# Head of a one-core hybrid decoder kernel: squares on two engines, scaling in pieces of 256 columns, the conv state turned between the x tiles

## Chip, cores and metric

The kernel runs on one core of one Trainium2 chip. The metric is the device time in microseconds of one execution.

## The reference, cut to what matters

One layer for 512 prompt tokens and 64 sample tokens (8 sequences of 8), width 1024, all in float32. Only its first lines are touched by the change:

```
h = rmsnorm(x, norm1_w)             # x * rsqrt(mean(x*x) + eps) * w, per token
proj = h @ w_in                     # 1024 wide in, 9248 wide out
q, k, v, z, xbc, dt, ga, gb = split(proj)
xbc, conv_new = causal_conv(xbc, conv_state, conv_w, conv_b)   # needs the last 3 rows of 8 sequences, 3072 channels
...                                 # stick-breaking attention over the paged cache, SSD scan, gates,
...                                 # output projection, SwiGLU feed-forward
```

Each float32 product is computed as three products of split operands, hi times hi, hi times lo and lo times hi.

## The kernel before

Each engine has its own program; they meet only in semaphores. Tokens lie in five tiles: four of 128 prompt tokens (x0 to x3) and one of 64 sample tokens (x4), in `x_tok`. Products have weights as the stationary operand, in chunks of 128 output columns, and the whole x (`x_hi`, `x_lo`: 8 slices of 128 rows by 576 tokens) as the moving one, so all of x must be squared, scaled and turned before the first chunk of weights can be finished. That start is the part that the change touches.

- SyncE issues the loads of x0 to x4, then the chunks of w_in (512 KB each); chunk 2 waits until chunk 0 has been split (`split`).
- ScalarE first issues 13 small loads on its own DMA queue: nine of parameters (`par_in`), `d_rows`, two of `dt_par`, and the conv state `sc_rows` (24 rows of 3072). Then it loads its table, squares x0 to x4 with the sum along the row, and makes `stats[:, 2]`, the inverse root per token.
- VectorE scales each x tile by it (1024 columns in one instruction, `x_scaled`).
- TensorE turns the parameters, then the 24 slices of the conv state into two spare banks ("conv_in"), then x. For each k of 8 it turns slice k of the five tiles into two of the four spare banks (I call these five matmuls turn k), ScalarE makes `x_hi` and VectorE `x_lo` from the banks with the norm weight from `par`, and TensorE multiplies slice k-1 with chunk 0 (six matmuls, `first_tile`; I call them product k-1). Turn k+2 needs the banks of turn k. So one turn is under way while the one before is being split.
- `make_hi(c)` on ScalarE and `make_lo(c)` on VectorE split weight chunk c; tile c needs them.

After product 7 come tile 1 with chunk 1, and all the rest of the program (attention with the gate weights as filler, the SSD groups, output and feed-forward), which this change leaves as it is except for a shift by two in the turn of the four spare banks.

Of the kernel before, what the change touches and what calls it, by code (L numbers as in the profile page):

```python
# [16 lines left out]
ALU = mybir.AluOpType  # L17
ACT = mybir.ActivationFunctionType

P = 128  # L20
D = 1024
# [104 lines left out]
def build(nc, x_prompt, x_sample, cache_k, cache_v, page_table, state_ssm, state_conv, norm1_w, w_in,  # L126
# [32 lines left out]
    with ExitStack() as ctx:  # L159
# [231 lines left out]
        keys = [("par", 0), ("par", 1), ("conv_in", 0), ("conv_in", 1)]  # L391
# [341 lines left out]

        sem_const_first, sem_const_all = [], []
# [3 lines left out]
        def _(sp_eng):  # L738
# [10 lines left out]
            for c in range(N_FIRST):  # L749
                load_chunk(eng, first_src(c), c, width=P if c < N_FIRST - 1 else NH)  # L750
            eng.dma_start(pages_sb[:, :], page_table.rearrange("b p -> (b p)").rearrange("(o n) -> o n", o=1)).then_inc(sem("pages_in"), 16)
# [73 lines left out]
        def _(pool):  # L825
# [195 lines left out]
            eng.wait_ge(sem("picks_made"), 1)  # L1021
# [88 lines left out]
        def _(pe):  # L1110
# [4 lines left out]
            pe.wait_ge(sem("par_in"), 16 * 9)  # L1115
            pe.transpose(spare(("par", 0))[:, 0:5 * CT], par_rows[:, :], ident[0:5 * CT, 0:5 * CT]).then_inc(bank_full[use[("par", 0)][0]], 1)
            pe.wait_ge(sem("d_spread"), 1)
            pe.transpose(spare(("par", 1))[:, 0:50], par2_rows[:, :], ident[0:50, 0:50]).then_inc(bank_full[use[("par", 1)][0]], 1)
            pe.wait_ge(sem("conv_state_in"), 16)
            for j in range(2):  # L1120
                for n in range(12):
                    ct = 12 * j + n
                    mm = pe.transpose(spare(("conv_in", j))[:, 24 * n:24 * n + 24], sc_rows[:, ct * P:(ct + 1) * P], ident[0:24, 0:24])
                mm.then_inc(bank_full[use[("conv_in", j)][0]], 1)
# [20 lines left out]

# [569 lines left out]
        def _(act):  # L1715
            eng = act

            eng.dma_start(par_rows[0:CW * CT, :], conv_w[0].rearrange("w (t p) -> (w t) p", p=P)).then_inc(sem("par_in"), 16)
# [6 lines left out]
            eng.dma_start(d_rows[32:48, :], d_skip[0].rearrange("(j e) -> j e", e=2)).then_inc(sem("d_in"), 16)  # L1725
            eng.dma_start(dt_par[:, 0:1], dt_bias[0].rearrange("(h o) -> h o", o=1)).then_inc(sem("dt_par_in"), 16)
            eng.dma_start(dt_par[:, 1:2], a_log[0].rearrange("(h o) -> h o", o=1)).then_inc(sem("dt_par_in"), 16)
            eng.dma_start(sc_rows[:, :], state_conv[0].rearrange("b t c -> (b t) c")).then_inc(sem("conv_state_in"), 16)

# [3 lines left out]
            for c, t0, m in token_tiles():  # L1733
                eng.wait_ge(sem(f"x_in{c}"), 16)
                junk = qo[0:m, 2 * c:2 * c + 2, 0:512]
                eng.activation(junk, x_tok[0:m, c, :].rearrange("p (a b) -> p a b", a=2), ACT.Square,
                               accum_out=stats[0:m, 0, c:c + 1]).then_inc(sem("x_rms"), 1)
# [3 lines left out]
            eng.activation(stats[:, 2, :], stats[:, 1, :], ACT.Exp, scale=-0.5).then_inc(sem("x_rms"), 1)  # L1741
            make_hi(0)
# [5 lines left out]
            for j in range(2):  # L1748
                key = ("conv_in", j)
                wait_full(eng, key)  # L1750
                eng.activation(conv_in[:, 12 * j:12 * j + 12, :].rearrange("p t n -> p (t n)"), spare(key)[:, 0:288], ACT.Copy)\
                   .then_inc(bank_read[use[key][0]], 1)
# [52 lines left out]
            for c in range(N_FIRST):  # L1805
                make_hi(c + 1, width=NH if c + 1 == N_FIRST - 1 else P, after_tiles=c if c else None)
                if 1 <= c <= KD + 2:
# [183 lines left out]
            for pick in picks:  # L1991
# [4 lines left out]
               .then_inc(sem("picks_made"), 1)  # L1996
# [338 lines left out]
        def _(dve):  # L2335
# [9 lines left out]

            eng.wait_ge(sem("d_in"), 16)
            eng.tensor_copy(par2_rows[32:48, :].rearrange("j (e p) -> j e p", e=2), d_rows[32:48, :].unsqueeze(2).to_broadcast([16, 2, HD]))\
               .then_inc(sem("d_spread"), 1)
            eng.wait_ge(sem("x_rms"), 7)
            for c, t0, m in token_tiles():  # L2350
                eng.tensor_scalar(x_tok[0:m, c, :], x_tok[0:m, c, :], stats[0:m, 2, c:c + 1], None, ALU.mult).then_inc(sem("x_scaled"), 1)
            make_lo(0)
            for k in range(KD):
                for j in range(2):
                    key = ("x", k, j)
                    eng.wait_ge(sem("x_hi_made"), 2 * k + j + 1)
# [661 lines left out]
```

## Time and profile before

| | us |
|---|---|
| median of 3 runs (lowest, highest) | 1417.89 (1417.79, 1418.38) |
| the profiled execution | 1418.91 |
| its span from first to last instruction | 1417.4 |
| TensorE matmul busy | 1351.2 (95%) |
| VectorE busy | 963.0 (68%) |
| ScalarE busy | 707.4 (50%) |
| GpSimd busy | 263.5 (19%) |

The profiled execution is 1.0 us above the median, and 1.5 us of it lie outside the span. All times of rows are counted from the start of the span. TensorE is busy in nearly every slice after the first; it does nothing in the first 10 us.

### The profile page before, as it was taken

The page shows a single profiled execution, that of the slowest core. Times are in us where ns is not written, and L with a number is a line of the kernel's source. Part 1 is how long each engine was busy: PE and PEld are TensorE (multiplying, and loading weights), DVE is VectorE, ACT ScalarE, POOL GpSimd, SP SyncE. Part 2 cuts the span into 40 slices and gives each one's busy share as a digit, 9 for nine tenths or more (in the row PEclk, how much of TensorE's full clock was granted, in tenths as well). Part 3 has the DMA queues.
Part 4 walks back from the last instruction along what each step waited for, and adds up shares of the span by engine and source line. Part 5 has one row for each costly group of instructions (what it writes and reads, how often), then busy time and mean ns, then how long its engine had stood idle before and what let it go on. Part 6 is the DMA issues. An engine that isn't in the chain of part 4 may idle for free. (4 is left out here: it accounts for less than half of the span.)

```text
span 1417.4 us, 26926 instructions
## 1 busy us (share of the span) xinstructions
PE 1351.2 (95%) x10301; PEld 1257.5 (89%) x10301; DVE 963.0 (68%) x1569; ACT 707.4 (50%) x1271; POOL 263.5 (19%) x467
## 2 busy tenths in 40 slices
PE   5999999999999899999999999999999999999996
PEld 4998777899999898888888887899999999999996
DVE  4455546788853476787787776877899999983221
ACT  4576445777632354574464464535644444452221
POOL 4002233000021423333333324211100000000000
PEclk9999999999999999999999999999999999999998
DMA  4226665122255333334334425362333333323331
GB/s 122 75 77 193 180 209 163 56 71 71 71 159 166 75 86 109 95 96 116 107 95 124 109 68 176 111 204 75 90 90 90 104 105 90 90 71 98 97 95 36
DMA packets 200897, 152.86 MB, mean 108 GB/s; under 512 B 15529, under 2 KB 187585, under 8 KB 200720
## 3 DMA queue, kind: packets, MB, share of 16 engines
q1 hardware_dynamic: 175394, 97.93, 24.5%
q0 software_dynamic: 24992, 52.85, 12.7%
q8 instruction: 83, 1.36, 0.4%
q10 hardware_dynamic: 384, 0.37, 0.1%
q14 instruction: 44, 0.35, 0.1%
HBM read 127.80 MB, written 23.29 MB: 107 GB/s over the span
## 5 line engine op out<-in xcount | busy, mean ns | idle before, releaser
L487 PE MATMUL tile_banks<-x_hi,w_hi 128*128 128x288 f32 (+1 forms) x1232 | 368.1, 314 | 11.5 <-DVE w_lo L461 10.1
L488 PE MATMUL tile_banks<-x_lo,w_hi 128*128 128x288 f32 (+1 forms) x1104 | 309.7, 296 | 0.0
L491 PE MATMUL tile_banks<-x_hi,w_lo 128*128 128x288 f32 (+1 forms) x1232 | 262.4, 294 | 0.0
L487 PEld LDWEIGHTS tile_banks<-x_hi,w_hi 128*128 128x128 f32 (+1 forms) x1232 | 231.7, 188 | 25.2 <-DVE w_lo L461 12.4
L461 DVE TENSOR_TENSOR w_lo<-w_raw,w_hi 128x1024 fp32r<-128x1024 f32 (+2 forms) x125 | 150.5, 1204 | 113.0 <-ACT w_hi L455 112.4
L488 PEld LDWEIGHTS tile_banks<-x_lo,w_hi 128*128 128x128 f32 (+1 forms) x1104 | 207.7, 188 | 5.5 <-issue 3.6
L491 PEld LDWEIGHTS tile_banks<-x_hi,w_lo 128*128 128x128 f32 (+1 forms) x1232 | 197.5, 187 | 0.4
L455 ACT ACTIVATE w_hi<-w_raw 128x1024 fp32r<-128x1024 f32 (+2 forms) x125 | 129.5, 1036 | 99.2 <-PE tile_banks L491 94.0
L488 PE MATMUL tile_banks<-f_lo,w_hi 128*128 128x288 f32 x352 | 98.6, 294 | 0.0
L1102 POOL DMA_DIRECT2D out_y_prompt<-y_tok x8 | 6.2, 778 | 386.1 <-ACT y_tok L2315 373.3
L2203 ACT ACTIVATE w_hi<-sum_raw 128x512 fp32r<-128x512 f32 x71 | 44.9, 634 | 60.3 <-PE tile_banks L1674 24.6
L488 PEld LDWEIGHTS tile_banks<-f_lo,w_hi 128*128 128x128 f32 x352 | 66.1, 188 | 0.0
L2572 DVE SCALAR_TENSOR_TENSOR conv_acc<-conv_src,conv_par,conv_acc 128x600 f32<-128x600 f32 x72 | 62.1, 862 | 2.5
L886 POOL DMA_DIRECT2D v_page<-in_cache_v x64 | 34.4, 537 | 154.4 <-issue 154.4
L487 PE MATMUL tile_banks<-y_hi,w_hi 128*128 128x288 f32 x192 | 56.1, 308 | 0.3 <-DVE w_lo L461 0.3
L487 PE MATMUL tile_banks<-t_blocks,w_hi 128*128 128x288 f32 x192 | 54.7, 300 | 1.6 <-DVE f_lo L2931 1.5
L488 PE MATMUL tile_banks<-y_lo,w_hi 128*128 128x288 f32 x192 | 53.8, 295 | 0.0
L2836 DVE TENSOR_TENSOR w_lo<-sum_raw,w_hi 128x512 fp32r<-128x512 f32 x71 | 49.9, 703 | 5.5 <-ACT w_hi L2203 5.5
L2031 ACT ACTIVATE conv_src<-tile_banks 128x288 f32<-128x288 f32 x24 | 9.9, 411 | 87.2 <-PE tile_banks L491 87.2
L2437 DVE TENSOR_TENSOR_SCAN after_w<-rest,zero_col 128x128 f32<-128x128 f32 (+2 forms) x64 | 52.3, 817 | 0.3
L1064 POOL DMA_DIRECT2D out_ssm_sample<-old x32 | 25.5, 797 | 118.1 <-DVE old L2717 108.0
L2439 DVE TENSOR_TENSOR beta<-beta,after_w 128x512 f32<-128x512 f32 (+2 forms) x80 | 42.6, 532 | 2.8
(490 smaller groups left out, 3678.1 us busy)
## 6 DMA issues: line engine op xcount, KB each, us to landing
w_raw<-in_w_in SPq DMA_DIRECT2D x68, 512.0 KB, 4.0
k_page<-in_cache_k SPq DMA_DIRECT2D x64, 128.0 KB, 2.6
v_page<-in_cache_v POOLq DMA_DIRECT2D x64, 128.0 KB, 3.0
old<-in_state_ssm POOLq DMA_DIRECT2D x32, 256.0 KB, 3.5
out_ssm_sample<-old POOLq DMA_DIRECT2D x32, 256.0 KB, 2.9
w_raw<-in_w_pb SPq DMA_DIRECT2D x16, 512.0 KB, 3.5
w_raw<-in_w_down SPq DMA_DIRECT2D x16, 512.0 KB, 4.0
gates_dram<-gate_out POOLq DMA_DIRECT2D x22, 288.0 KB, 2.8
```

Source lines behind the costliest of these rows:

```text
L455: nc.scalar.activation(w_hi[:, c % 2, 0:tiles, 0:width], w_raw[:, c % 2, 0:tiles, 0:width], ACT.Copy).then_inc(hi_made, 1)
L461: nc.vector.tensor_tensor(w_lo[:, c % 2, 0:tiles, 0:width], w_raw[:, c % 2, 0:tiles, 0:width], f32(w_hi[:, c % 2, 0:tiles, 0:width]), ALU. ...
L487: nc.tensor.matmul(out, wh, xh[:, HALVES[h]], start=start and k == 0, stop=False, skip_group_check=onto)
L488: nc.tensor.matmul(out, wh, xl[:, HALVES[h]], start=False, stop=False, skip_group_check=onto)
L491: mm = nc.tensor.matmul(out, wl, xh[:, HALVES[h]], start=False, stop=stop and k == last, skip_group_check=onto)
L886: eng.dma_start(v_page[:, n % V_SLOTS, :], cache_v[0, bass.ds(page_of(eng, x, k), 1)].rearrange("o p h d -> p (o h d)")).then_inc(sem(f"v_ ...
L1064: eng.dma_start(states_of(ssm_sample, g, b), old[:, b % 2]).then_inc(sem(f"state_stored{b % 2}"), 16)
L2203: eng.activation(form_slot(f)[0], form_raw(f), ACT.Copy).then_inc(sem("form_hi_made"), 1)
L2437: link(eng.tensor_tensor_scan(out=after_w[:, slot, edge - width:edge][:, ::-1], data0=rest[:, slot, cols][:, ::-1], data1=zero_col[:, 0:1] ...
L2439: return eng.tensor_tensor(beta[:, x["u"] % 4, cols], beta[:, x["u"] % 4, cols], after_w[:, slot, edge - width + 1:edge + 1], ALU.mult)
L2572: ins = eng.scalar_tensor_tensor(out=dst, in0=src[:, w:w + m], scalar=conv_par[:, w * CT + ct:w * CT + ct + 1], in1=dst, op0=ALU.mult, op1 ...
L2836: eng.tensor_tensor(low, form_raw(f), f32(high), ALU.subtract).then_inc(sem("form_split"), 1)
```

## The change

ScalarE squares x0, x2, x4 and VectorE x1, x3. Scaling is cut in pieces of 256 columns (two slices): pieces of x3 and x4 on ScalarE, of x0 to x2 on VectorE, the first ones before turn 0, the next ones after slices 0, 2 and 4 have been split. Turn 0 comes before the parameters' turns. The conv state's turns go to the idle product banks `G[1]`, four behind each of turns 2 to 7; their copies to `conv_in` stand behind the split of chunk 1, and tile 1 waits for them. The loads of the conv state and of `dt_par` move from ScalarE's queue to SyncE's, behind weight chunk 1, and `d_rows` becomes ScalarE's first load. One semaphore is replaced by another count of an existing one.

```
             for c in range(N_FIRST):
                 load_chunk(eng, first_src(c), c, width=P if c < N_FIRST - 1 else NH)
+                if c == 1:
+                    eng.dma_start(sc_rows[:, :], state_conv[0].rearrange("b t c -> (b t) c")).then_inc(sem("conv_state_in"), 16)
+                    eng.dma_start(dt_par[:, 0:1], ...).then_inc(sem("dt_par_in"), 16)
+                    eng.dma_start(dt_par[:, 1:2], ...).then_inc(sem("dt_par_in"), 16)
...
@@ TensorE @@
+            def turn_conv_state(cts):
+                pe.wait_ge(sem("conv_state_in"), 16)
+                for ct in cts:
+                    n = ct % 12
+                    mm = pe.transpose(conv_state_bank(ct // 12)[:, 24 * n:24 * n + 24], sc_rows[:, ct * P:(ct + 1) * P], ident[0:24, 0:24])
+                    if n == 11:
+                        mm.then_inc(sem("conv_state_turned"), 1)
...
-                        if k == 0:
-                            pe.wait_ge(sem("x_scaled"), c + 1)
+                        if k % 2 == 0:
+                            pe.wait_ge(sem("x_scaled"), 5 * (k // 2 + 1))
...
+                if k == 0:
+                    turn_par()
+                if k >= 2:
+                    turn_conv_state(range(4 * (k - 2), 4 * (k - 1)))
                 if k:
                     first_tile(k - 1)
             first_tile(KD - 1).then_inc(tile_done, 1)
+            pe.wait_ge(sem("conv_state_in"), CONV_STATE_READ)
...
@@ ScalarE @@
             for c, t0, m in token_tiles():
+                if c not in SQUARES_ACT:
+                    continue
...
+            def scale_columns(k):
+                for c, t0, m in token_tiles():
+                    if c in SCALED_ACT:
+                        cols = slice(k * P, k * P + SCALE_COLS)
+                        eng.activation(x_tok[0:m, c, cols], x_tok[0:m, c, cols], ACT.Copy, scale=stats[0:m, 2, c:c + 1]).then_inc(sem("x_scaled"), 1)
+            eng.wait_ge(sem("x_rms"), 7)
+            scale_columns(0)
             make_hi(0)
...
+                if k % 2 == 0 and k + 2 < KD:
+                    scale_columns(k + 2)
...
@@ VectorE @@
+                if c in SQUARES_DVE:
+                    eng.wait_ge(sem(f"x_in{c}"), 16)
+                    eng.scalar_tensor_tensor(out=qo[...], in0=x_tok[0:m, c, :], scalar=1.0, in1=x_tok[0:m, c, :],
+                                             op0=ALU.mult, op1=ALU.mult, accum_out=stats[0:m, 0, c:c + 1]).then_inc(sem("x_rms"), 1)
...
-                eng.tensor_scalar(x_tok[0:m, c, :], x_tok[0:m, c, :], stats[0:m, 2, c:c + 1], None, ALU.mult).then_inc(sem("x_scaled"), 1)
+                        eng.tensor_scalar(x_tok[0:m, c, cols], x_tok[0:m, c, cols], stats[0:m, 2, c:c + 1], None, ALU.mult).then_inc(sem("x_scaled"), 1)
```

TensorE, from its first instruction to the first products. Before:

```order
L1116 MATMUL spare_bank<-ident,par_rows 128x120 [waits par_in,constants]
L1118 MATMUL spare_bank<-ident,par_rows 128x50 [waits d_spread]
L1123 MATMUL spare_bank<-ident,sc_rows 128x24 [waits conv_state_in]
L1123 MATMUL spare_bank<-ident,sc_rows 128x24 x23
L1140 MATMUL spare_bank<-ident,x_tok 128x128 [waits x_scaled,bank_read0]
```

Of the change, the same place, and on to product 1:

```order
L1157 MATMUL spare_bank<-ident,x_tok 128x128 [waits x_scaled,constants]
L1157 MATMUL spare_bank<-ident,x_tok 128x128 [waits x_scaled] x3
L1157 MATMUL spare_bank<-ident,x_tok 128x64 [waits x_scaled]
L1131 MATMUL spare_bank<-ident,par_rows 128x120 [waits par_in]
L1133 MATMUL spare_bank<-ident,par_rows 128x50 [waits d_spread]
...
L1157 MATMUL spare_bank<-ident,x_tok 128x128 [waits x_scaled,bank_read2]
L1157 MATMUL spare_bank<-ident,x_tok 128x128 [waits x_scaled] x3
L1157 MATMUL spare_bank<-ident,x_tok 128x64 [waits x_scaled,bank_read3]
L1139 MATMUL tile_banks<-ident,sc_rows 128x24 [waits conv_state_in]
L1139 MATMUL tile_banks<-ident,sc_rows 128x24 x3
L487 MATMUL tile_banks<-x_hi,w_hi 128x288 [waits weights_split,bank_read1,bank_read0]
```

The 24 turns of the conv state left the place ahead of turn 0; four stand now between a turn and the product behind it, six times.

ScalarE, from the table load to the second slice. Before:

```order
L1731 ACT_TABLE_LOAD
L1736 ACTIVATE qo,stats<-x_tok 128x2x512 [waits x_in0,constants]
...
L1741 ACTIVATE stats<-stats 128x5 [waits x_rms]
L455 ACTIVATE w_hi<-w_raw 128x1024 [waits weights_in0]
L1747 ACTIVATE conv_par<-spare_bank 128x120 [waits bank_full0]
L1747 ACTIVATE par<-spare_bank 128x50 [waits bank_full1]
L1751 ACTIVATE conv_in<-spare_bank 128x288 [waits bank_full2]
L1751 ACTIVATE conv_in<-spare_bank 128x288 [waits bank_full3]
L1759 ACTIVATE x_hi<-spare_bank,par 128x512 [waits bank_full0,bank_read1]
```

Of the change:

```order
L1761 ACTIVATE stats<-stats 128x5 [waits x_rms]
L1767 ACTIVATE x_tok<-x_tok,stats 128x256 [waits x_rms]
L1767 ACTIVATE x_tok<-x_tok,stats 64x256
L455 ACTIVATE w_hi<-w_raw 128x1024 [waits weights_in0]
L1776 ACTIVATE conv_par<-spare_bank 128x120 [waits bank_full0]
L1776 ACTIVATE par<-spare_bank 128x50 [waits bank_full1]
L1783 ACTIVATE x_hi<-spare_bank,par 128x512 [waits bank_full2,bank_read1]
L1783 ACTIVATE x_hi<-spare_bank,par 128x64 [waits bank_full3]
L1767 ACTIVATE x_tok<-x_tok,stats 128x256
L1767 ACTIVATE x_tok<-x_tok,stats 64x256
L1783 ACTIVATE x_hi<-spare_bank,par 128x512 [waits bank_full0]
```

Two scaling pieces stand now ahead of the first weights and two behind the first slice; the copies of the conv state are gone from here.

## Rows read from the trace of the kernel before

**Rows 1.** The page, its head line.
```profile
span 1417.4 us, 26926 instructions
```
**Rows 2.** Loads of x3 and x4 (issue starts; issue to landing, least and most).
```profile
L741 SPq DMA_DIRECT2D x_tok<-in_x_prompt x1: 432/432/432, 2.5 to 2.5; - x1
L742 SPq DMA_DIRECT2D x_tok<-in_x_sample x1: 568/568/568, 2.9 to 2.9; - x1
...
DMA to landing us min/median/max: 7.8/8.5/9.2
```
**Rows 3.** Load of weight chunk 0, the same columns.
```profile
L445 SPq DMA_DIRECT2D w_raw<-in_w_in x1: 594/594/594, 3.5 to 3.5; - x1
...
DMA to landing us min/median/max: 12.0/12.0/12.0
```
**Rows 4.** Timeline of ScalarE in the head (start us, us, engine, line, what).
```profile
5.12 0.76 ACTq L1726 DMA_DIRECT2D dt_par<-in_dt_bias  x1
...
7.13 1.28 ACT L1731 ACT_TABLE_LOAD   x1 [7.13 <-issue]
...
12.60 1.04 ACT L1736 ACTIVATE qo<-x_tok 64x1024 fp32r<-64x1024 f32 x1
...
15.57 1.06 ACT L455 ACTIVATE w_hi<-w_raw 128x1024 fp32r<-128x1024 f32 x1 [1.27 <-DMA w_raw<-in_w_in]
...
16.69 0.20 ACT L1747 ACTIVATE par<-spare_bank 128x50 f32<-128x50 f32 x1
16.78 0.41 ACT L1751 ACTIVATE conv_in<-spare_bank 128x288 f32<-128x288 f32 x1
...
18.92 0.89 ACT L1759 ACTIVATE x_hi<-spare_bank,par 128x512 fp32r<-128x512 f32 x2 [0.69 <-PE spare_bank L1140]
```
**Rows 5.** Timeline of VectorE in the head.
```profile
14.34 3.39 DVE L2351 TENSOR_SCALAR x_tok<-x_tok,stats 128x1024 f32<-128x1024 f32 x5 [2.25 <-ACT stats L1741]
...
19.64 0.94 DVE L2359 SCALAR_TENSOR_TENSOR x_lo<-spare_bank,par,x_hi 128x512 fp32r<-128x512 f32 x2 [0.78 <-ACT x_hi L1759]
```
**Rows 6.** Timeline of TensorE's weight loads, conv state to product 2.
```profile
15.02 2.63 PEld L1123 LDWEIGHTS spare_bank<-ident,sc_rows 24*128 24x128 f32 x24 [2.71 <-DMA sc_rows<-in_state_conv]
17.70 0.71 PEld L1140 LDWEIGHTS spare_bank<-ident,x_tok 128*128 128x128 f32 x4
...
20.65 0.29 PEld L487 LDWEIGHTS tile_banks<-x_hi,w_hi 128*128 128x128 f32 x1 [0.39 <-DVE x_lo L2359]
...
22.06 0.85 PEld L1140 LDWEIGHTS spare_bank<-ident,x_tok 128*128 128x128 f32 x4
...
23.43 0.19 PEld L487 LDWEIGHTS tile_banks<-x_hi,w_hi 128*128 128x128 f32 x1
...
24.21 0.49 PEld L1140 LDWEIGHTS spare_bank<-ident,x_tok 128*128 128x128 f32 x4
24.87 0.14 PEld L1140 LDWEIGHTS spare_bank<-ident,x_tok 64*128 64x128 f32 x1 [0.17 <-issue]
25.07 0.19 PEld L487 LDWEIGHTS tile_banks<-x_hi,w_hi 128*128 128x128 f32 x1
```
**Rows 7.** Timeline, slice 4 on its way to product 4.
```profile
26.61 0.89 ACT L1759 ACTIVATE x_hi<-spare_bank,par 128x512 fp32r<-128x512 f32 x2 [0.74 <-PE spare_bank L1140]
...
27.33 0.94 DVE L2359 SCALAR_TENSOR_TENSOR x_lo<-spare_bank,par,x_hi 128x512 fp32r<-128x512 f32 x2 [0.69 <-ACT x_hi L1759]
...
28.35 0.19 PEld L487 LDWEIGHTS tile_banks<-x_hi,w_hi 128*128 128x128 f32 x1
```
**Rows 8.** Timeline, from the split of chunk 1 to tile 1.
```profile
32.31 1.06 ACT L455 ACTIVATE w_hi<-w_raw 128x1024 fp32r<-128x1024 f32 x1
...
33.60 1.22 DVE L461 TENSOR_TENSOR w_lo<-w_raw,w_hi 128x1024 fp32r<-128x1024 f32 x1
...
34.87 0.19 PEld L487 LDWEIGHTS tile_banks<-x_hi,w_hi 128*128 128x128 f32 x1 [0.77 <-DVE w_lo L461]
```
**Rows 9.** Busy time by stretch: PE, PEld, DVE, ACT, POOL, granted clock, DMA share, GB/s.
```profile
478.00:482.00 4.00, 4.00 (x23) 4.00 (x23) 0.00 (x0) 0.22 (x1) 3.07 (x7) 0.68 0.70 163
```

More of the change, by code:

```diff
@@ L388, in build @@
         gates_dram = nc.dram_tensor("gates_dram", (N_FILL, P, T), F32, kind="Internal").ap()
-        keys = [("par", 0), ("par", 1), ("conv_in", 0), ("conv_in", 1)]
+        keys = [("par", 0), ("par", 1)]
         keys += [("x", k, j) for k in range(KD) for j in range(2)]
@@ L732, in f_low, with conv_state_bank @@
             return f_lo[:, k, :]
+        SCALE_COLS = 2 * P
+        SQUARES_ACT, SQUARES_DVE = (0, 2, 4), (1, 3)
+        SCALED_ACT, SCALED_DVE = (3, 4), (0, 1, 2)
+        CONV_STATE_READ = 16 + 2
+        def conv_state_bank(j):
+            return G[1][:, j, 0:12 * 24]
         sem_const_first, sem_const_all = [], []
@@ L750, in _ @@
                 load_chunk(eng, first_src(c), c, width=P if c < N_FIRST - 1 else NH)
+                if c == 1:
+                    eng.dma_start(sc_rows[:, :], state_conv[0].rearrange("b t c -> (b t) c")).then_inc(sem("conv_state_in"), 16)
+                    eng.dma_start(dt_par[:, 0:1], dt_bias[0].rearrange("(h o) -> h o", o=1)).then_inc(sem("dt_par_in"), 16)
+                    eng.dma_start(dt_par[:, 1:2], a_log[0].rearrange("(h o) -> h o", o=1)).then_inc(sem("dt_par_in"), 16)
             eng.dma_start(pages_sb[:, :], page_table.rearrange("b p -> (b p)").rearrange("(o n) -> o n", o=1)).then_inc(sem("pages_in"), 16)
@@ L1020, in _ @@
                 sums_in(st)
-            eng.wait_ge(sem("picks_made"), 1)
+            eng.wait_ge(sem("sums_hi_made"), 3)
             for g in range(2):
@@ L1113, in _, with turn_par @@
             pe.wait_ge(sem("constants"), sem_const_first[0])
[L1115 to L1124, printed above, removed]
+            def turn_par():
+                pe.wait_ge(sem("par_in"), 16 * 9)
+                pe.transpose(spare(("par", 0))[:, 0:5 * CT], par_rows[:, :], ident[0:5 * CT, 0:5 * CT]).then_inc(bank_full[use[("par", 0)][0]], 1)
+                pe.wait_ge(sem("d_spread"), 1)
+                pe.transpose(spare(("par", 1))[:, 0:50], par2_rows[:, :], ident[0:50, 0:50]).then_inc(bank_full[use[("par", 1)][0]], 1)
+            def turn_conv_state(cts):
[5 more added lines that the diff above has]
+                        mm.then_inc(sem("conv_state_turned"), 1)
             def first_tile(k):
@@ L1716, in _ @@
             eng = act
+            eng.dma_start(d_rows[32:48, :], d_skip[0].rearrange("(j e) -> j e", e=2)).then_inc(sem("d_in"), 16)
             eng.dma_start(par_rows[0:CW * CT, :], conv_w[0].rearrange("w (t p) -> (w t) p", p=P)).then_inc(sem("par_in"), 16)
@@ L1724, in _ @@
                     eng.dma_start(par2_rows[at:at + 1, e * HD:(e + 1) * HD], w).then_inc(sem("par_in"), 16)
[L1725 to L1728, printed above, removed]
             eng.preload_act_table_set("natural_log_exp_and_others")
@@ L1733, in _ @@
             for c, t0, m in token_tiles():
+                if c not in SQUARES_ACT:
+                    continue
                 eng.wait_ge(sem(f"x_in{c}"), 16)
-                junk = qo[0:m, 2 * c:2 * c + 2, 0:512]
+                junk = qo[0:m].rearrange("p a t -> p (a t)")[:, c * D:(c + 1) * D].rearrange("p (a b) -> p a b", a=2)
                 eng.activation(junk, x_tok[0:m, c, :].rearrange("p (a b) -> p a b", a=2), ACT.Square,
@@ L1747, in _ @@
                 eng.activation(dst[:, :], spare(key)[:, 0:n], ACT.Copy).then_inc(bank_read[use[key][0]], 1)
[L1748 to L1752, printed above, removed]
             wait_after_read(eng, ("par", 1))
@@ L1806, in _ @@
                 make_hi(c + 1, width=NH if c + 1 == N_FIRST - 1 else P, after_tiles=c if c else None)
+                if c == 0:
+                    for j in range(2):
+                        eng.wait_ge(sem("conv_state_turned"), j + 1)
+                        eng.activation(conv_in[:, 12 * j:12 * j + 12, :].rearrange("p t n -> p (t n)"), conv_state_bank(j), ACT.Copy)\
+                           .then_inc(sem("conv_state_in"), 1)
                 if 1 <= c <= KD + 2:
@@ L1995, in _ @@
             eng.activation(pair_picks[used, :].rearrange("p (e d) -> p e d", e=2), pair_rows[used, 0:2].unsqueeze(2).to_broadcast([SEG_ROWS, 2, HD]), ACT.Copy)\
-               .then_inc(sem("picks_made"), 1)
+               .then_inc(sem("sums_hi_made"), 1)
             def conv_silu(key):
@@ L2344, in link, with scale_columns @@
                 eng.wait_ge(chain, n_chain[0])
+            eng.wait_ge(sem("constants"), sem_const_first[0])
+            for c, t0, m in token_tiles():
+                if c in SQUARES_DVE:
+                    eng.wait_ge(sem(f"x_in{c}"), 16)
+                    eng.scalar_tensor_tensor(out=qo[0:m].rearrange("p a t -> p (a t)")[:, c * D:(c + 1) * D], in0=x_tok[0:m, c, :], scalar=1.0,
+                                             in1=x_tok[0:m, c, :], op0=ALU.mult, op1=ALU.mult,
+                                             accum_out=stats[0:m, 0, c:c + 1]).then_inc(sem("x_rms"), 1)
+            def scale_columns(k):
+                for c, t0, m in token_tiles():
+                    if c in SCALED_DVE:
+                        cols = slice(k * P, k * P + SCALE_COLS)
+                        eng.tensor_scalar(x_tok[0:m, c, cols], x_tok[0:m, c, cols], stats[0:m, 2, c:c + 1], None, ALU.mult).then_inc(sem("x_scaled"), 1)
+            eng.wait_ge(sem("x_rms"), 7)
+            scale_columns(0)
             eng.wait_ge(sem("d_in"), 16)
@@ L2348, in _ @@
                .then_inc(sem("d_spread"), 1)
-            eng.wait_ge(sem("x_rms"), 7)
-            for c, t0, m in token_tiles():
-                eng.tensor_scalar(x_tok[0:m, c, :], x_tok[0:m, c, :], stats[0:m, 2, c:c + 1], None, ALU.mult).then_inc(sem("x_scaled"), 1)
             make_lo(0)
@@ L2360, in _ @@
                                              in1=f32(x_hi[:, k, cols]), op0=ALU.mult, op1=ALU.subtract).then_inc(bank_read[use[key][0]], 1)
+                if k % 2 == 0 and k + 2 < KD:
+                    scale_columns(k + 2)
             wait_after_read(eng, ("par", 1))
```

## Prediction

> **What bounds the kernel now.** I read the page first, then the timeline of the first 40 us engine by engine, then the landings of single loads. The span is 1417.4 us [rows 1], and TensorE is busy nearly all of it once it has begun, so a microsecond by which tile 1 starts earlier is a microsecond of the whole, and only the time up to tile 1, which starts at 34.87 [rows 8], is at stake. I call the five x turns of slice k "turn k" and the six matmuls of first_tile(k) "product k", as above.
>
> Three chains meet there. (a) ScalarE loads its table at 7.13, behind its DMA issues, and squares five tiles back to back at 1.04 each; the last starts at 12.60, and scaling can start 1.74 later, at 14.34; VectorE needs 3.39 for it, to 17.73 [rows 4, 5]. (b) TensorE waits for the conv state until 15.02 and turns it in 2.63, and begins turn 0 at 17.70, so (a) and (b) end together [rows 5, 6]. (c) Weight chunk 0 lands at 3.5 + 12.0 = 15.5, is split to hi at 15.57 [rows 3, 4]. Then x_hi of slice 0 starts at 18.92, x_lo at 19.64, and product 0 at 20.65 [rows 4 to 6].
>
> From there a loop: product 0 starts at 20.65, product 1 at 23.43, product 2 at 25.07, product 4 at 28.35 [rows 6, 7], which is 1.64 each; so product 7 is at 28.35 + 3 x 1.64 = 33.27, and tile 1 follows 1.6 later behind the low part of chunk 1 (1.22) [rows 8]. Two things set the 1.64 at once. TensorE has 0.78 for a product (23.43 to 24.21) and 0.86 for a turn (24.21 to 25.07) [rows 6], together all of it. And a slice takes from turn to product 24.21 to 26.71, 2.5 us (a turn's start to x_hi about 0.77, x_hi to x_lo 0.72, x_lo to product 1.02 [rows 6, 7]); with the 0.78 of the product ahead of the turn that is 3.28 for two slices. So TensorE has no free time in the loop: whatever is put in there is paid.
>
> **The change, part by part.** *Start of scaling.* Three DMA issues leave ScalarE, so the table load moves from 7.13 to 5.12, and it ends at 6.4 [rows 4]. Three squares then wait for data, not for the engine. The last needs x4, which landed at 2.9 + 9.2 = 12.1, though x3, twice its size, landed at 2.5 + 7.8 = 10.3 [rows 2]. The conv state and dt loads that now shared the DMA engines with it come after it. Bounds: 12.1, nothing gained, and 10.3, with x3. I take 11.0. Scaling starts 1.74 later, 12.75. VectorE's squares of x1 and x3 are not in the trace; 0.94 for 576 columns [rows 5] makes at most 1.7 for 1024, so the one of x3 is over at 12.0, covered by x4's 1.04 and the roots; if x4 came with x3 it would be late by some 0.6.
>
> *First pieces.* VectorE, three of 256 columns: a whole tile takes 3.39/5 = 0.68, a quarter of it 0.17 without overhead; I take 0.25 each, 0.75. ScalarE, two: 288 columns took 0.41 [rows 4], so at most 0.8. Turn 0 starts at 13.5, 4.2 before the old one.
>
> *To product 0.* Turn 0 takes 1.37 at the slow clock (22.06 to 23.43), then the parameters' two turns, two matmuls where turn 0 has five, so 0.55, and a gap: 15.6. ScalarE copies them (0.20 for par), so x_hi at 15.85 and product 0 by 1.73 later (18.92 to 20.65 [rows 4, 6]): 17.6. The other chain is chunk 0: landing, 1.06, 1.22, 1.01 and small gaps. It must land by 14.2 not to bind. It landed at 15.5 behind the same competitors; I take 13.5. With 15.5 product 0 would be at 18.9. So product 0 gains 3.0, bounds 1.7 and 4.2.
>
> *The conv turns.* 24 turns in 2.63, 0.11 each at the slow clock [rows 6]. Ahead of turn 0 they go away (part of the 3.0). Behind turns 2 to 7 four stand each time in a loop without slack. Their price at the full clock is unknown: product and turn went from 1.41 (20.65 to 22.06) and 1.37 to 0.78 and 0.86 [rows 6], so 0.055 to 0.11 each, 0.22 to 0.44 for four; and the change from 128-row to 64-row turns costs a gap of 0.17 (24.87) [rows 6], which 64 to 24 rows may cost again. Per loop 0.2 to 0.6; I take 0.35: 0.07 a turn and half of the gap, for a group that may overlap its neighbours. The first comes ahead of product 1, at the slow clock, 0.6. The loss up to product 7 is 0.6 and four times 0.35 (turns 3 to 6; that behind turn 7 delays product 6, which has 0.8 to spare), 2.0; bounds 1.2 and 3.0.
>
> *The clock.* Matmuls are at half rate (1.2 GHz) in product 0 and turn 2, and at the full rate (2.4) from product 1 on [rows 6]: 1.41 against 0.78 for the same six. Before the rise there had been turns from 15.02 and products from 20.65; it came between 22.06 and 23.43, some 2.5 us after the first product. If it again follows the products by 2.5 it comes at 20.1, when turn 2 is about over: product 0 at 17.6, turn 2 at 19.0, conv turns 20.4, product 1 at 21.0, gain 2.4, of which the slow clock takes nothing more. If it follows the turns (8.1 after 15.02, so 21.6 after a start at 13.5), product 1 is mostly slow, 0.4 lost. If it stays at 23.2, product 1 and turn 3 are slow, 0.6 + 0.5 = 1.1 lost. I take the first. The Trainium skill (TensorE: Matmul & The Clock Gate, Part 4: PE-mode transpose) says that transposes don't count as TensorE being busy; by that rule the rise goes with the products, the sum as above, against 0.4 less if turns counted. The trace agrees in that 5 us of turns did not raise it.
>
> *Scaling pieces in the loop.* VectorE 0.75 behind x_lo of slices 0, 2, 4: it idles 0.69 there [rows 7] and the loop is now 0.35 longer. ScalarE 0.75, idle 0.74 [rows 7], the same. Turn k+2 comes after product k, 0.78 after x_lo, when the pieces are done. Nothing, up to 0.1 each if the loop were not longer.
>
> *The rest.* The conv copies, 2 x 0.41, stand behind the hi part of chunk 1 (32.31 to 33.37) and end at 34.2, 0.65 before tile 1 [rows 4, 8], which waits for them: nothing; they would cost at 1.5 each. SyncE's three issues more stand ahead of chunk 2, which waits for the split of chunk 0 anyway. The shift in the banks and the semaphore count cost nothing: the spare banks are used in the same turn with the same distances.
>
> **Sum.** +3.0 at product 0, less 0.6 ahead of product 1 and 1.4 in the loop: gain 1.0. The profiled execution's 1418.9 would become 1417.9; against the median, 1.0 below it, 1417.89 becomes 1416.9.
>
> **The rivals.**
> - *B, the loads come much earlier:* x4 at 10.3 or before, chunk 0 by 13, turns at 0.055 without a gap. Product 0 gains 4.2, the loop takes 1.2: gain 2 to 3.4, 1415.9 to 1414.5. For it: x4 is half a tile and landed 1.8 behind x3 [rows 2]. Against: SyncE's own weights stand right behind x4 in its queue.
> - *C, the loads come as before:* x4 at 12.1, chunk 0 at 15.5. Product 0 gains 1.7, the loop takes 2.0 less what its clock, at the same distance from the products, gives back at the edge of turn 2: gain 0 within 0.4, 1417.9. The change's sense would be lost. For it: whatever is behind x4 now was not proved to be the conv state.
> - *D, slower:* the clock does not rise by the end of the first short products, because they are now spread between turns, at 3.4 or more instead of 2.8 us. A rise at 23.2 takes 1.1, and the conv groups at 0.6 another 4 x 0.25 = 1.0: 1.0 - 1.1 - 1.0 = -1.1, so 1419.0. The sign turns with a rise at about 23.2; each further microsecond at the slow clock costs about 0.45 (1.41 against 0.78), so beyond 0.2% it needs a rise after 27.
> - *E, 478 to 482:* TensorE has a granted clock of 0.68 there after an idle stretch [rows 9], about 1.3 us lost. If the earlier arrival moves that stretch it may go or grow: 1415.6 or 1418.2.
>
> **How the numbers follow.** Forecast (gain 0.3 to 1.8) 0.50, B 0.26, C 0.11, D 0.09, E 0.04. 0.2% is 2.84 us, about what a measurement of this kernel can tell from no change. Of B half is beyond it, 0.13, with a little of E: faster 0.15. Of D a third: slower 0.03. Same 0.82. The range leaves out the upper part of B and the far part of D: 1415.0 to 1418.5.
>
> **What would show it.** Table load at about 5.1; last square at 11.0 (step 1 right) or 12.1 (C); turn 0 at 13.5; product 0 at 17.6; products 2.0 apart instead of 1.64 (the conv turns); full rate from 20 on; product 7 at about 32.3, tile 1 at 33.9. Wrong if the loop stays at 1.64 (then the gain is 2.5 or more), or if tile 1 waits for the conv copies.

## The result, and the profile after

The kernel after the change takes 1425.05 us (median of 7 runs, 1423.81 to 1429.29), the one before 1417.89 (7 runs, 1416.74 to 1420.20). The ratio is 1.0052, with a 95% interval of 1.0041 to 1.0063: **slower by 0.5%**, where 1416.9 was forecast, with 0.03 for slower. The profiled execution took 1424.49 with the span below, 5.6 us more than before [rows 1]. Single executions of before and of experiments 7, 8 and 10 took 1497 to 3608 us, where all others of one kernel lie within 12 us of each other; the ratios leave them out. The page of after, its head line:

```profile
span 1423.0 us, 26946 instructions
```

Timeline of ScalarE in the head of after (start, us, engine, line, what); it answers to [rows 4]:

```profile
5.22 1.28 ACT L1749 ACT_TABLE_LOAD   x1 [5.22 <-issue]
...
11.02 1.06 ACT L1756 ACTIVATE qo<-x_tok 64x1024 fp32r<-64x1024 f32 x1 [2.29 <-DMA x_tok<-in_x_sample]
...
12.77 0.91 ACT L1767 ACTIVATE x_tok<-x_tok,stats 128x256 f32<-128x256 f32 x2
13.58 1.04 ACT L455 ACTIVATE w_hi<-w_raw 128x1024 fp32r<-128x1024 f32 x1
...
16.15 0.89 ACT L1783 ACTIVATE x_hi<-spare_bank,par 128x512 fp32r<-128x512 f32 x2
```

All of this came close to the forecast: the square of x4 at 11.0 (11.0), the first pieces at 12.77 (12.75), x_hi of slice 0 at 16.15 (15.85). The timeline of TensorE's weight loads in after, which answers to [rows 6 to 8]; the rows shown are the first of product 0, turn 2, the first conv turns, products 1, 2 and 7, and tile 1:

```profile
17.88 0.29 PEld L487 LDWEIGHTS tile_banks<-x_hi,w_hi 128*128 128x128 f32 x1 [0.70 <-DVE x_lo L2404]
...
19.29 0.85 PEld L1157 LDWEIGHTS spare_bank<-ident,x_tok 128*128 128x128 f32 x4
20.47 0.18 PEld L1157 LDWEIGHTS spare_bank<-ident,x_tok 64*128 64x128 f32 x1 [0.33 <-issue]
20.77 0.50 PEld L1139 LDWEIGHTS tile_banks<-ident,sc_rows 24*128 24x128 f32 x4
21.32 0.29 PEld L487 LDWEIGHTS tile_banks<-x_hi,w_hi 128*128 128x128 f32 x1
...
24.76 0.29 PEld L487 LDWEIGHTS tile_banks<-x_hi,w_hi 128*128 128x128 f32 x1
...
39.89 0.33 PEld L487 LDWEIGHTS tile_banks<-x_hi,w_hi 128*128 128x128 f32 x1
...
41.33 0.33 PEld L487 LDWEIGHTS tile_banks<-x_hi,w_hi 128*128 128x128 f32 x1
...
42.05 0.27 PEld L488 LDWEIGHTS tile_banks<-x_lo,w_hi 128*128 128x128 f32 x1
...
42.53 0.19 PEld L487 LDWEIGHTS tile_banks<-x_hi,w_hi 128*128 128x128 f32 x1
42.66 0.19 PEld L488 LDWEIGHTS tile_banks<-x_lo,w_hi 128*128 128x128 f32 x1
```

Product 0 is 2.77 earlier than before (20.65 to 17.88), product 1 still 2.11 (23.43 to 21.32). Then products stand 3.44 apart until the end of the loop: 21.32 + 5 x 3.44 = 38.52 for product 6. A product takes 1.41 (17.88 to 19.29), as product 0 did before [rows 6]: TensorE stays at its low level, 1.2 GHz, through the whole loop in this execution. Only in the middle of tile 1, when products follow one another without turns, do the starts go from 0.24 to 0.13 apart (42.53 to 42.66), which is the 2.4 GHz level. Tile 1 starts at 41.33, 6.46 later than before [rows 8].

The sum of the rows is exact: +2.77 at product 0, -0.66 ahead of product 1, -8.73 from product 1 to product 7 (18.57 for 9.84), and +0.16 from product 7 to tile 1 (1.44 for 1.60), is -6.46. Busy time by stretch, in after, the columns of [rows 9]:

```profile
17.80:21.30 3.50, 3.38 (x15) 2.92 (x15) 1.65 (x6) 1.52 (x5) 1.38 (x4) 1.00 0.44 116
21.30:39.80 18.50, 18.50 (x81) 15.89 (x81) 7.51 (x21) 7.34 (x17) 0.00 (x0) 1.00 0.00 1
```

In 18.5 us the profile shows no idle time of TensorE's matmuls (18.50 of 18.50; their ends are modelled, and the weight loads have one gap of 0.33 in each slice), and still it runs at the low level. The column of the granted clock prints 1.00 there: ahead of the first rise it doesn't show the level, and one has to read it from the spacing of equal instructions. After the first rise it does show falls.

What is lost in the head is most of the difference. The gate and gated outputs leave on POOL's queue; of these groups of DMA issues (least, median and most ns, then first to last issue), first two of before, then two of after:

```profile
L905 POOL DMA_DIRECT2D gates_dram<-gate_out x22: 540/542/569, 133.1 to 401.6; - x22
L935 POOL DMA_DIRECT2D gated_dram<-gate_out x8: 544/546/552, 416.9 to 457.9; - x8
```

```profile
L918 POOL DMA_DIRECT2D gates_dram<-gate_out x22: 540/542/569, 139.8 to 407.8; - x22
L948 POOL DMA_DIRECT2D gated_dram<-gate_out x8: 544/544/549, 422.4 to 462.6; - x8
```

The lateness is 6.7 at 133, 6.2 at 402, 5.5 at 417, 4.7 at 458 and 5.6 at the end. So up to 1.8 of the 6.5 us are taken up on the way, and 0.9 of the span in the end. These are two single executions, and experiment 1 shows that one execution can gain or lose 2 to 3 us behind the head.

### The profile page after: what moved, and what is told of

Its sections match the earlier page's. It is cut to its first block and busy times, and to the rows that moved or that the text cites. A ratio compares the mean times of both kernels' runs of the same rounds, so it can differ in the third digit from the quotient of the medians.

```text
span 1423.0 us, 26946 instructions
## 1 busy us (share of the span) xinstructions
PE 1359.3 (96%) x10301; PEld 1264.6 (89%) x10301; DVE 965.8 (68%) x1580; ACT 708.5 (50%) x1275; POOL 263.9 (19%) x467
```

## The experiments

**Theory 1**, formed from the profile above: the conv turns lengthen the slow slice from 2.78 [rows 6] to 3.44, of which only 1.41 is products, and the clock doesn't rise in such a loop. **Theory 2:** it is the unbroken stretch of turns right ahead of product 0 (15.02 to 20.65 before) that lets the clock rise soon after, and the change took it away. **Theory 3:** the scaling pieces or the short last square are what slows the loop. "Constants" below are fp32 matmuls of the tile of ones by the identity into an unused part of a bank, whose result nobody reads; all conv turns are still made.

**Experiment 1: all conv turns behind the loop.** The rest of the change stays.

```
-                if k >= 2:
-                    turn_conv_state(range(4 * (k - 2), 4 * (k - 1)))
...
             first_tile(KD - 1).then_inc(tile_done, 1)
+            turn_conv_state(range(0, 24))
```

> The change, with all 24 conv turns behind product 7 instead of four behind each of turns 2 to 7. Theory 1 (the conv turns thin out the products so far that the clock does not rise in the loop): the clock rises within 2 to 6 us of product 0 at about 17.9, tile 1 starts between 32 and 35, and the time is 1415 to 1418.5. Theory 2 (what raised the clock before was the long unbroken run of turns ahead of product 0, which the change took away): the clock stays low through the loop, period 2.8, tile 1 at about 39 to 41, 1422 to 1425. Theory 3 (the scaling pieces and their waits in the loop) says the same as theory 2.

Measured: 1419.42 (12 runs, 1415.86 to 1423.38, in two groups, up to 1418.2 and from 1420.7), beside 1417.82 of before; ratio 1.0013 (1.0001 to 1.0024). The profiled execution took 1416.2. Its timeline of weight loads (product 7, the conv turns, tile 1):

```profile
30.45 0.19 PEld L487 LDWEIGHTS tile_banks<-x_hi,w_hi 128*128 128x128 f32 x1 [0.81 <-DVE x_lo L2403]
...
31.45 1.55 PEld L1139 LDWEIGHTS tile_banks<-ident,sc_rows 24*128 24x128 f32 x24 [0.16 <-issue]
33.60 0.19 PEld L487 LDWEIGHTS tile_banks<-x_hi,w_hi 128*128 128x128 f32 x1 [0.60 <-ACT conv_in L1835]
```

Product 1 came 2.89 behind product 0 (17.46 to 20.35), the clock rose within it, 3.6 behind product 0, and stayed up for the loop; product 7 stands at 30.45, 9.4 earlier than in after. So neither the missing turns ahead of product 0 (theory 2) nor the scaling pieces (theory 3) hold it down: both are as in after here. But the clock falls again, in the windows of the same kernel:

```profile
31.00:34.60 3.60, 3.10 (x35) 2.83 (x35) 1.68 (x2) 1.87 (x4) 0.00 (x0) 1.00 0.40 104
34.60:38.00 3.40, 3.40 (x17) 3.40 (x15) 1.23 (x1) 0.47 (x1) 0.00 (x0) 0.50 0.27 69
```

What TensorE did ahead of the fall was 24 conv turns and some idle time (31.45 to 33.60). Through it all of the 1.3 us by which tile 1 is earlier than before is gone: the first matmuls on `conv_out` start at 41.41, in before at 41.18. The clock and tile 1 came as theory 1 expected, the median (1415 to 1418.5) didn't. What separates the two groups is not shown, since the traced execution has this fall and lies in the lower group; its 2.7 us less than before's traced one come from behind the head.

**Experiment 2: only the conv turns' move, in the kernel before.** Squares, scaling and loads as before; the turns go into the loop by the line that experiment 1 takes out, and the copies of conv_in behind make_hi(1).

> The kernel before, with the conv turns alone moved as in the change (four behind each of turns 2 to 7, copies behind the split of chunk 1); squares, scaling and loads as before. Theory 1: product 0 at about 20, the clock stays low, period 3.44, tile 1 at about 42 to 43.5, 1425 to 1428. Theory 2: the same direction, since here too the 24 turns ahead of turn 0 are gone. Theory 3: the clock rises by 24, product to product 1.9, 1418 to 1420.

Measured: 1427.03 (1425.36 to 1428.41), ratio 1.0064 (1.0052 to 1.0076). This part alone costs at least what the whole change does; the medians lie 2 us apart, and the intervals overlap. Weight loads (product 0, conv turns, product 1):

```profile
19.24 0.29 PEld L487 LDWEIGHTS tile_banks<-x_hi,w_hi 128*128 128x128 f32 x1 [0.48 <-DVE x_lo L2364]
...
22.13 0.50 PEld L1124 LDWEIGHTS tile_banks<-ident,sc_rows 24*128 24x128 f32 x4
22.68 0.29 PEld L487 LDWEIGHTS tile_banks<-x_hi,w_hi 128*128 128x128 f32 x1
```

Again 3.44 apart, and the low level until about 44.9, by the spacing. Tile 1 is at 42.69.

**Experiment 3: after, with 24 constants ahead of turn 0.**

```
             pe.wait_ge(sem("constants"), sem_const_first[0])
+            for n in range(24):
+                pe.matmul(G[1][:, 0, 0:128], ones[:, :], ident[:, :])
```

> The change, with 24 float32 matmuls of constants (ones by ident, 128x128, into an idle bank, never read) in TensorE's idle time ahead of turn 0. If the clock is all that went wrong, turns 0 and 1 and all products run at the full rate: product 0 at 17.0 to 17.5, products about 1.9 to 2.0 apart, tile 1 at 31.5 to 33, time 1413.5 to 1416.5. If the share of products in the loop is also too small to keep the clock up, it falls again within the loop and tile 1 comes after 36.

Measured: 1426.28 (1424.33 to 1427.79), ratio 1.0055 (1.0043 to 1.0067): no gain. Its weight loads and windows:

```profile
3.42 7.71 PEld L1128 LDWEIGHTS tile_banks<-ident,ones 128*128 128x128 f32 x48 [3.42 <-POOL conv_out L848]
13.68 0.42 PEld L1159 LDWEIGHTS spare_bank<-ident,x_tok 128*128 128x128 f32 x4 [2.55 <-DVE x_tok L2392]
...
15.16 0.72 PEld L1159 LDWEIGHTS spare_bank<-ident,x_tok 128*128 128x128 f32 x4 [0.29 <-ACT conv_par L1778]
```

```profile
15.00:18.40 3.40, 2.78 (x11) 2.29 (x11) 3.21 (x8) 2.69 (x8) 2.76 (x11) 0.51 0.38 101
```

The constants raised the clock: four turn loads take 0.42 at 13.68, for 0.71 at the low level [rows 6]. Then TensorE waited 2.55 and made turns, and at 15.0 the clock was down (0.51), ahead of product 0. So the loop started at the low level, with its slices 3.44 apart; the expectation had the clock fall within the loop at the earliest. A clock that is high early is worth nothing if turns and idle time stand between it and the products.

**Experiment 4: half of the conv turns in the loop.** Two behind each of turns 2 to 7, twelve behind product 7.

> The change, with two conv turns behind each of turns 2 to 7 and twelve behind product 7. The slow loop would be about 3.2 us a slice instead of 3.44. Theory 1: between the two: either the clock rises late in the loop (tile 1 at 35 to 38, 1418 to 1422) or not at all (tile 1 at about 40, 1423 to 1425). Theory 2 and 3: as the change, 1423 to 1425.

Measured: 1426.81 (1424.78 to 1432.08), ratio 1.0069 (1.0051 to 1.0086). Slices of 3.23, tile 1 at 42.28, low until about 48.2; tile 1 and the time lie above both expected ranges. Two turns were enough to keep the clock down; that the 12 behind product 7 moved its rise from 42.2 to 48.2 fits experiment 1.

**Experiment 5: two constants more in each loop of after.** The slice grows, but by matmuls.

```
                 if k >= 2:
+                    for n in range(2):
+                        pe.matmul(G[1][:, 1, 288:416], ones[:, :], ident[:, :])
                     turn_conv_state(range(4 * (k - 2), 4 * (k - 1)))
```

> The change with all its conv turns in the loop, and two more float32 matmuls of constants (128x128, never read) ahead of each group of four. This makes the slow loop longer still (about 4.0 us a slice) but gives products about half of TensorE's time again, as in the kernel before. Theory 1 in its form 'what counts is the share of products, turns do not count': the clock rises in the loop, within 6 us of product 0, in spite of the longer loop. Theory 1 in its form 'a loop longer than so much keeps it down', or if anything that makes TensorE do more between products is bad: the clock stays low, tile 1 at 44 or later, 1428 or more.

Measured: 1426.01 (4 runs, 1422.24 to 1426.34), ratio 1.0052 (1.0037 to 1.0067); the profiled execution took 1422.24. Its weight loads around the rise (constants, conv turns, product 2, product 3):

```profile
24.97 0.93 PEld L1163 LDWEIGHTS tile_banks<-ident,ones 128*128 128x128 f32 x4
26.12 0.32 PEld L1139 LDWEIGHTS tile_banks<-ident,sc_rows 24*128 24x128 f32 x4 [0.23 <-issue]
26.48 0.19 PEld L487 LDWEIGHTS tile_banks<-x_hi,w_hi 128*128 128x128 f32 x1
...
29.11 0.19 PEld L487 LDWEIGHTS tile_banks<-x_hi,w_hi 128*128 128x128 f32 x1
```

The clock rose at 26.1, in the loop, 8.6 behind product 0 (expected: within 6), although product 2 stands 4.40 behind product 1 (22.08). So in this execution the clock rose in a longer slice than that of after, with more matmuls that aren't turns in it. The constants cost 0.64 a slice at the high level too (2.63 for the 1.99 of experiment 9), so the rise gives little back: 1422.24 beside 1424.49. But the other three executions took 3.5 to 4.1 more and have no trace. An estimate: a clock that stays low from product 2 to product 6 costs 7.1 (four slices at 4.40 for 2.63), so they fit a rise about two slices later, which is not shown.

**Experiments 6 to 8: other places for the 24 turns.** 6 puts six behind each of turns 4 to 7; 7 puts 12 ahead of product 0 and 12 behind product 7, into a spare bank; 8 puts all 24 ahead of product 0, behind turn 1. The line that changes, in 6, 7 and 8 in turn:

```
+                if k >= 4:
+                    turn_conv_state(range(6 * (k - 4), 6 * (k - 3)))
...
+                if k == 1:
+                    turn_conv_state(range(0, 12))
...
+                if k == 1:
+                    turn_conv_state(range(0, 24))
```

> The change with the conv turns put behind turns 4 to 7 only, six each, when the clock should be up already. If a thin loop only prevents the rise: the clock rises at 21 to 24 and stays, period about 2.1 at the full rate, tile 1 at 33 to 34.5, 1416 to 1418.5. If it also takes the clock down again once it is up: a fall between 26 and 35, tile 1 after 35, 1419 to 1424.

> The change with 12 conv turns in TensorE's idle time ahead of product 0 and 12 in its idle time ahead of tile 1, these into a spare bank so that tile 1 does not wait for their copy. Theory 1: product 0 at 18.4 to 18.8, clock up at 21 to 24 and no fall after product 7, tile 1 at 32 to 33, 1415 to 1416.5. If the clock falls behind product 7 as in the run with 24 there: 1417 to 1421, in two groups.

> The change with all 24 conv turns between turn 1 and product 0, none in the loop. Theory 1: product 0 at about 19.8, clock up within 2 to 5 us of it, tile 1 at 33.5 to 34.5, 1416 to 1418. No group of slow executions, since nothing stands between product 7 and tile 1.

Measured (12 runs each, before 1418.65): 1418.37, ratio 1.0001 (0.9987 to 1.0015); 1418.45, 1.0002 (0.9991 to 1.0013); 1419.28, 1.0001 (0.9991 to 1.0011). All are level with before. Tile 1 starts at 35.20, 35.90 and 35.03, later than expected in all three, and the medians of 7 and 8 lie above their ranges. Experiment 6 shows best what theory 1 says; its weight loads, and a window over slices with six turns each:

```profile
27.74 0.44 PEld L1139 LDWEIGHTS tile_banks<-ident,sc_rows 24*128 24x128 f32 x6
28.21 0.19 PEld L487 LDWEIGHTS tile_banks<-x_hi,w_hi 128*128 128x128 f32 x1
```

```profile
24.00:36.00 12.00, 11.26 (x87) 9.78 (x87) 7.73 (x19) 6.87 (x16) 0.00 (x0) 1.00 0.01 1
```

Products 0 to 2 have no conv turns ahead of them; they start 2.89 apart at first, and the clock rises among them, between 22.93 and 23.80. Six turns a slice then cost 0.46 (2.10 for 1.64) and don't bring it down: a loop with more turns than that of after, which couldn't raise the clock, keeps it up. In 7, whose slow slices are as short (2.89), it rose only at 27.9, 9.4 behind product 0, as its weight loads show (product 3 and turn 5):

```profile
27.17 0.29 PEld L487 LDWEIGHTS tile_banks<-x_hi,w_hi 128*128 128x128 f32 x1
...
28.27 0.49 PEld L1157 LDWEIGHTS spare_bank<-ident,x_tok 128*128 128x128 f32 x4
```

In 8 it rose at 24.4, 4.3 behind; before, some 2.5 behind. So even the short slice raises it after a time that varies. The traced executions of 7 and 8 also show a fall of some 3.4 us later on (from about 420.5 and 174.2), at places where no kernel here was changed.

**Experiment 9: the change as it is, with constants right up to product 0.**

```
+            constants(32)
...
+                if k == 1:
+                    constants(4)
                 if k >= 2:
```

> The change as it is, conv turns in the loop, with 32 float32 matmuls of constants ahead of turn 0 (up to about 13.5) and four in TensorE's idle time ahead of product 0. Theory 1, with what the run with the turns behind turns 4 to 7 showed (once up, the clock stays up in a thin loop): clock up at 7 to 11, no fall before tile 1, product 0 at 17.0 to 17.4, slices about 1.95 apart, tile 1 at 31.5 to 33, time 1414 to 1417: all of the change's loss is the clock. If it falls ahead of product 0 as in the run with 24 constants: 1424 to 1427 again.

Measured: 1417.06 (12 runs, 1413.82 to 1419.35), at the upper end of what was expected, beside 1418.9 of before; ratio 0.9984 (0.9973 to 0.9995). Its weight loads (constants, product 0, conv turns, products 1 and 2):

```profile
15.66 0.97 PEld L1131 LDWEIGHTS tile_banks<-ident,ones 128*128 128x128 f32 x8
16.73 0.19 PEld L487 LDWEIGHTS tile_banks<-x_hi,w_hi 128*128 128x128 f32 x1
...
18.36 0.32 PEld L1146 LDWEIGHTS tile_banks<-ident,sc_rows 24*128 24x128 f32 x4
18.72 0.19 PEld L487 LDWEIGHTS tile_banks<-x_hi,w_hi 128*128 128x128 f32 x1
...
20.71 0.19 PEld L487 LDWEIGHTS tile_banks<-x_hi,w_hi 128*128 128x128 f32 x1
```

With the clock up from the start the change's own loop runs at 1.99 a slice, product 7 is at 29.97 and tile 1 at 31.59, 9.7 earlier than in after. The two kernels differ in nothing but the constants: the way from a ratio of 1.0052 to one of 0.9984 is the clock's. That is 9.6 us, as the 9.7 of tile 1; the medians lie 8.0 apart, but each stands beside other runs of before (1417.89 and 1418.9). The change kept warm is 1.8 us faster than before, which starts at the low level itself, and 2.2 faster than before kept warm (experiment 10, by the medians).

**Experiment 10: the kernel before, kept warm in the same way** (38, 3 and 2 constants in its gaps).

> The kernel before with the same idea and nothing else: 38 float32 matmuls of constants ahead of the parameters' turns, three behind the conv turns, two ahead of product 0. Clock up from 7 to 11 on; product 0 at about 20, slices 1.64 apart, tile 1 at 32.5 to 33.5, 1415.5 to 1417: a gain of 1.5 to 2.5 without any part of the change.

Measured: 1419.3 (12 runs, 11 of them 1416.23 to 1424.07), ratio 1.0007 (0.9994 to 1.002). The profiled execution took 1416.33, 2.6 less than that of before; product 0 is at 20.10 and tile 1 at 33.15, 1.7 earlier. The head came as expected, and the median shows nothing of it. There is one hint: the mean granted clock is 0.996 in the traced execution, which has the clock up from the constants on, and 0.991 to 0.992 in the three slowest (1422.48 to 1424.07), where before has 0.993 to 0.996. That points to falls elsewhere in these executions, but where they are is not shown, and the execution of 1419.9 has 0.991 as well.

**Experiment 11: the split turns of 7, kept warm** (32 constants ahead of turn 0, two behind the 12 conv turns).

> The change with its conv turns split (12 ahead of product 0, 12 ahead of tile 1) and 32 constants ahead of turn 0, two ahead of product 0. Clock up from 7 to 11 on and not down again; product 0 at about 17.2, slices 1.64 apart, tile 1 at 30.3 to 31.5, 1412.5 to 1415: 3 to 5 us faster than the kernel before. If the clock falls ahead of product 0: 1418 to 1421.

Measured: 1415.64 (12 runs), ratio 0.9979 (0.9966 to 0.9991). The profiled execution took 1418.09, and in it the clock fell once more ahead of product 0 (18.91; tile 1 at 33.17), the case for which 1418 to 1421 was expected; the first conv turns, and the window:

```profile
17.05 1.00 PEld L1146 LDWEIGHTS tile_banks<-ident,sc_rows 24*128 24x128 f32 x12 [0.71 <-DMA sc_rows<-in_state_conv]
```

```profile
16.00:21.00 5.00, 4.43 (x29) 4.06 (x28) 2.84 (x8) 2.18 (x6) 2.47 (x9) 0.66 0.42 110
```

Ahead of it TensorE had waited 0.71 for the conv state, now behind the first weights in its queue, and made 12 turns.

**Experiment 12: late turns, kept warm.** Constants as in 9 (34 and 4), six conv turns behind turns 6 and 7 each, twelve behind product 7 in a spare bank as in 7.

```
+                if k >= 6:
+                    turn_conv_state(range(6 * (k - 6), 6 * (k - 5)))
```

> The change with 34 constants ahead of turn 0 and four ahead of product 0, its conv turns six each behind turns 6 and 7 and twelve ahead of tile 1 in a spare bank. If the clock is the whole story: up at 7 to 11 and no fall before tile 1, product 0 at 16.7 to 17.3, slices 1.64 apart up to product 4, tile 1 at 30 to 31, 1412.5 to 1415.5, the fastest of all. If a loop of 1.64 has hidden costs in the early start: tile 1 as in the run with four turns each, 31.6, 1417.

Measured: **1414.46** (10 runs, 1413.38 to 1416.11), beside 1417.6 of before; ratio 0.9978 (0.9969 to 0.9988). It has the lowest median and the narrowest runs; by the ratio it is level with experiment 11. Its weight loads (first constants, product 0, product 7, the last conv turns, tile 1):

```profile
3.43 9.54 PEld L1131 LDWEIGHTS tile_banks<-ident,ones 128*128 128x128 f32 x68 [3.43 <-POOL conv_out L848]
...
17.20 0.19 PEld L487 LDWEIGHTS tile_banks<-x_hi,w_hi 128*128 128x128 f32 x1
...
29.15 0.19 PEld L487 LDWEIGHTS tile_banks<-x_hi,w_hi 128*128 128x128 f32 x1 [0.34 <-DVE x_lo L2419]
...
30.14 0.82 PEld L1177 LDWEIGHTS spare_bank<-ident,sc_rows 24*128 24x128 f32 x12 [0.17 <-issue]
30.99 0.19 PEld L487 LDWEIGHTS tile_banks<-x_hi,w_hi 128*128 128x128 f32 x1
```

Tile 1 starts 3.9 earlier than before [rows 8]; of the span 4.0 are gone (1413.4), in the median 3.1.

## Why the prediction was wrong

**Up to product 0 it held.** Table load 5.22 (forecast 5.12), the last square 11.02 (11.0), scaling 12.77 (12.75), ScalarE's pieces 0.91 (at most 0.8), VectorE's 0.90 (0.75), product 0 at 17.88 (17.6): a gain of 2.77 for the 3.0 forecast. Chunk 0 didn't bind: its split followed the pieces at once, at 13.58 (13.5). That the sum came out this close is in part luck: the same head starts the square of x4 at 10.51 to 11.76 and product 0 at 17.46 to 18.64 in the traces of after and of experiments 1, 4, 5 and 6.

**The conv turns' price held too.** At the low level four cost 0.55 (20.77 to 21.32; forecast 0.6), and at the high level 0.35 (experiment 9: 1.99 for 1.64; forecast 0.35). Between the 64-row turn and the 24-row turns no gap is shown: the row at 20.77 in after has no idle time ahead of it. Over the loop with the clock up, from product 1 to product 7, they cost 11.25 (18.72 to 29.97) less the 9.84 of before, 1.41; forecast 1.4.

**The step that failed** is the one on the clock, "I take the first": a rise at 20.1, 2.5 us behind product 0, as before. It didn't come until 42.1. Of the 8.73 lost between products 1 and 7, 1.41 are the turns and the other 7.32 the low level. The argument took the distance from the first product to the rise as fixed, and so counted the turns as free for the clock, where they stretch the time between products. What decided, in these traces, was what stood between the products: with 1.41 of products in slices of 2.78 (before) and 2.89 (1, 6, 7, 8) the clock rose within the loop; with 1.41 in 3.23 (4) and in 3.44 (after, 2, 3) it didn't, in some 22 us; with constants added to the products it rose even in a slice of 4.40 (5, in the one execution that was traced). That the turns themselves count for nothing, or for less, is the reading which fits all of these, but a direct comparison of turns with equally long idle time wasn't run.

The forecast had weighed a rule against the rows here: the Trainium skill (TensorE: Matmul & The Clock Gate, Part 4: PE-mode transpose) says that transposes don't count as TensorE being busy in the same way. The runs agree with it, after's 18.5 us without idle time above all; the mistake was to use it only for when the rise would come, and not for whether it would.

**Rival D had the mechanism**, "the clock does not rise by the end of the first short products, because they are now spread between turns", with a chance of 0.09 and a loss of 1.1, for a rise at 23.2. Both were too low. (It also says that the sign turns with a rise at about 23.2; by its own sum the change is 1.1 slower there already.) For a later rise it gave a rate, 0.45 a microsecond, and the latest rise that it names is 27; by that rate a rise at 42.1 gives 1427.5 (1419.0 + 18.9 x 0.45). Nothing in the trace of before bounded the rise, and the far case wasn't worked out. It comes from the forecast's own sum, with the slow slice that the runs show: product 1 to product 7 takes 18.57 instead of 11.3, 7.3 more, which moves 1416.9 to 1424.2. Measured: 1425.05.

**B, C and E** didn't come: the square of x4 started with its landing at 11.02, and chunk 0 held nothing up. The low stretch of E is there in both traces and as long in both, some 3.4 us: from 477.1 to 480.5 in before, and from 482.5 to 486 in after (granted clock 0.63 from 482 to 484, 0.52 from 484 to 486). It stands behind a wait of TensorE of 4.21 in before and 4.14 in after; in every traced kernel here this wait is 4.1 to 4.2 and the clock falls behind it. The forecast carried the head's gain to the end in full; of the loss of 6.5 in the head, 5.6 are left in the span of the traced execution.

**What stays open.** When the clock rises in a loop near the edge: 2.5 to 9.4 us behind product 0 with nearly the same slice. Each kernel's loop is seen in one execution, so that the loops of after and of experiment 4 stay low in the others too is known only from their times. Why experiment 10 is not faster in the median while its profiled execution is, and 11 and 12 are. And what decides on the single later falls of some 3.4 us, in the traces of 7, 8, 9 and 11. Each follows a wait of TensorE (2.27 up to 420.47 in 7, 1.82 up to 174.19 in 8, 1.80 up to 508.94 in 9, 2.18 up to 1020.08 in 11), but waits as long pass without a fall in the same and in other traces (2.18 up to 1026.88 in after, 2.63 up to 951.12 in 11).

## What to carry to other kernels

Small transposes put between short matmuls of a loop that starts cold can be paid twice: their own time, and the rise of the clock that may not come; put them where long runs of matmuls already hold the clock up, or into a stretch that waits anyway, though not many at once: 24 in such a stretch were followed by a fall (experiment 1), 12 were not (7 and 12).

Before a loop is counted at the full rate, ask what raises the clock in it, and price the case that nothing does. If a head waits for loads, matmuls of constants in its gaps, up to the first real product, can be what makes a reordering pay. Here neither did alone: the constants brought nothing to the kernel before (1419.3 for 1418.9, experiment 10), nor did the reordered heads without them (6 to 8); both together brought about 3 us (11, and 12 with 1414.5 for 1417.6).

## What was unexpected of the hardware

- TensorE without idle time by the profile for 18.5 us (21.30 to 39.80 in after) stayed at 1.2 GHz. The Trainium skill (TensorE: Matmul & The Clock Gate, Part 1) says that the clock rises with sustained matmul activity; this trace agrees only if the turns aren't taken as such activity.
- The level depends on the past: slices of 1.99 and 2.10 with 0.78 of products kept the clock up (experiments 6, 9, 12), slices of 3.44 with 1.41 of products didn't raise it. Turns and idle time did bring it down: 24 turns and 0.76 of idle time in experiment 1, where it fell about a microsecond later, within tile 1; turns and a wait of 2.55 in 3; 0.71 of waiting and 12 turns in 11. In experiment 10, 24 turns between constants (15.31 to 16.86) did not.
- A 24-row turn took 0.11 to 0.13 at the low level (2.63 for 24 before [rows 6], 0.50 for four in after), and 0.065 to 0.08 at the high one (1.55 for 24 in experiment 1, 0.32 for four in 9).
